# A hybrid decoder step on one core: order of the first loads, and who turns the sample rows

## The reference, cut to what matters

```python
def rms_norm(x, g):
    y = xf * lax.rsqrt(jnp.mean(xf * xf, axis=-1, keepdims=True) + RMS_EPS)
    return (y * g).astype(x.dtype)

h = rms_norm(xp, norm_g[l])                  # xp: 512 x 2048; the same for xs: 8 x 2048
z = jnp.einsum('btd,de->bte', h, w_in)       # w_in: 2048 x 6144
u, gp, q, k, v, ga = split(z)
pm = pool_mix(u, ...)                        # trailing means, a 256 x 256 map for each group
a = dilated_attn(q, k, v, ...)               # 16 heads of 64
xp = xp + concat(pm * silu(gp), a * silu(ga)) @ w_out
y = rms_norm(xp, final_norm_g)
```

## Time and profile before

| what | before |
|---|---|
| three runs, us | 821.51, 822.56, 828.95 |
| median, us | 822.56 |
| the profiled execution: its time, its span, us | 821.09, 819.3 |
| TensorE busy in the span | 807.1 us, 99% |
| VectorE, ScalarE, GpSimd busy | 77%, 49%, 25% |
| mean granted TensorE clock | 0.996 |

### The profile page before, as it was taken

One profiled execution on the slowest core, in us unless ns is written; L12 is line 12 of the kernel. 1 busy time (PEld: TensorE's weight loads), 2 busy tenths in 40 slices (PEclk: granted clock), 3 DMA queues, 4 the chain that ended last, 5 costly groups with the idle time before them and its releaser, 6 DMA issues.

```text
span 819.3 us, 17483 instructions
## 1 busy us (share of the span) xinstructions
PE 807.1 (99%) x6625; PEld 802.6 (98%) x6625; DVE 627.4 (77%) x1347; ACT 398.9 (49%) x875; POOL 203.2 (25%) x340
## 2 busy tenths in 40 slices
PE   9999999999999999999999999999999999999995
PEld 8999999999999999999999999999999999999994
DVE  4657895897589778958885897689888886777765
ACT  4745435533554454345435533553465345555554
POOL 2103502520360045014402610450000131222220
PEclk9999999999999999999999999999999999999998
DMA  8569647856774696578558756884668567766565
GB/s 297 142 173 232 168 125 171 231 144 168 188 208 122 163 233 169 152 175 228 152 141 186 204 147 182 193 214 123 172 195 272 156 181 203 207 184 174 150 180 218
DMA packets 271499, 150.04 MB, mean 183 GB/s; under 512 B 44448, under 2 KB 261472, under 8 KB 271392
## 3 DMA queue, kind: packets, MB, share of 16 engines
q1 hardware_dynamic: 239784, 118.97, 53.7%
q0 software_dynamic: 12672, 20.59, 9.9%
q10 hardware_dynamic: 18960, 9.38, 4.0%
HBM read 119.49 MB, written 28.27 MB: 180 GB/s over the span
## 4 chain that ended last, share of the span: by engine, by line
PE 87%; DVE 6%; DMA 3%; issue 1%; ACT 1%; SPq 1%; POOL 1%; DVEq 0%; ACTq 0%
PE pj L889 64%; PE pj L1048 13%; PE ps_s L946 1%; PE ps_s L948 1%; PE ps_o L977 1%; PE ps_o L975 1%; DMA out<-arena 1%; PE ps_o L889 1%; DVE w_lo L1624 1%; PE ps_t L995 1%; PE ps_s L995 1%; PE ps_s L889 1%; PE ps_s L827 1%; DVE arena L1755 1%; DMA w_raw<-in_w_out 0%
## 5 line engine op out<-in xcount | busy, mean ns | idle before, releaser
L889 PE MATMUL pj<-mov_hi,w_hi 128*128 128x260 f32 (+1 forms) x1632 | 332.1, 285 | 0.3 <-DVE mov_lo L1645 0.3
L889 PE MATMUL pj<-mov_hi,w_lo 128*128 128x260 f32 (+1 forms) x1632 | 328.3, 283 | 0.0
L889 PE MATMUL pj<-mov_lo,w_hi 128*128 128x260 f32 (+1 forms) x1632 | 327.8, 282 | 0.0
L889 PEld LDWEIGHTS pj<-mov_hi,w_hi 128*128 128x128 f32 x1632 | 252.7, 189 | 2.1 <-issue 0.6
L889 PEld LDWEIGHTS pj<-mov_lo,w_hi 128*128 128x128 f32 x1632 | 251.4, 188 | 0.0
L889 PEld LDWEIGHTS pj<-mov_hi,w_lo 128*128 128x128 f32 x1632 | 251.4, 188 | 0.0
L1148 ACT ACTIVATE w_hi<-w_raw 128x640 fp32r<-128x640 f32 (+1 forms) x157 | 121.4, 773 | 228.5 <-PE pj L889 159.3
L1624 DVE TENSOR_TENSOR w_lo<-w_raw,w_hi 128x640 fp32r<-128x640 f32 (+1 forms) x157 | 135.5, 863 | 62.7 <-ACT w_hi L1148 62.3
L1566 POOL DMA_DIRECT2D p_scratch<-extra x168 | 104.8, 631 | 82.4 <-DVE extra L1727 79.9
L1597 POOL DMA_DIRECT2D y_scratch<-arena x56 | 37.6, 678 | 110.5 <-DVE arena L2209 81.3
L1540 POOL DMA_DIRECT2D out<-arena x8 | 4.6, 569 | 213.0 <-DMA arena<-arena 213.0
(11 more groups left out here) (275 smaller groups left out, 1295.3 us busy)
## 6 DMA issues: line engine op xcount, KB each, us to landing
w_raw<-in_w_in SPq DMA_DIRECT2D x96, 320.0 KB, 4.1
w_raw<-in_w_in SPq DMA_DIRECT2D x48, 384.0 KB, 4.5
arena<-in_cache_k_win SPq DMA_DIRECT2D x16, 384.0 KB
arena<-in_cache_v_win SPq DMA_DIRECT2D x16, 384.0 KB
p_scratch<-extra POOLq DMA_DIRECT2D x112, 48.0 KB, 3.3
w_raw<-in_w_out SPq DMA_DIRECT2D x26, 192.0 KB, 3.0
arena<-in_cache_k_win SPq DMA_DIRECT2D x8, 512.0 KB
arena<-in_cache_v_win SPq DMA_DIRECT2D x8, 512.0 KB
```

Source lines behind the costliest of these rows:

```text
L889: mm = pe.matmul(dst[h][:, 0:own.stop - own.start], w, m[:, k, own], start=(k == 0 and i == 0), stop=(c == 2 and k == KT - 1 and i == 2))
```

## The change

Four things are changed, all of them in the opening.

1. Loads on SyncE: x piece 0 goes first. x is cut into eight pieces (1, 1, 2, 2, 2, 2, 3, 3 k's). Weight chunk 0 comes in two transfers, k's 0 and 1 with a semaphore of their own (`first_in`), k's 2 to 5 on `raw_in[0]`. Chunk 1 stands behind x piece 4, chunk 2 behind piece 6. The plain rows `x_smp` (which only a sum of squares needs in step 1) come last.
2. The gains and the samples are loaded by ScalarE's queue. The samples go into a block of zeros `smp_blk` (written by GpSimd) in four transfers that place 32-element pieces so that one VectorE transpose by 32x32 blocks gives all 16 k's turned (`smp_t`). TensorE's 16 sample transposes are gone.
3. On ScalarE and VectorE the samples' split now stands behind that of k = 0, not ahead of it.
4. On TensorE there are 7 + 2 + 3 + 2 matmuls on zeros where there were 11 + 2 + 8, some of them now between the turns of k = 0 and k = 1. k's 2, 3 are turned after the product of k = 1, k's 4, 5 after that of k = 2, and then x of k + 3 after the product of k.

Four semaphores of a later stage are used for the two added x pieces, for `first_in` and for `smp_in`; the later waits count 16 more (`mov_count`).

```diff
-        x_cols = tuple(P * k for k in (0, 2, 4, 6, 10, 13, 16))
+        x_at = (0, 1, 2, 4, 6, 8, 10, 13, 16)
+        x_cols = tuple(P * k for k in x_at)
...
-            sp.dma_start(ident, consts[:, C_ID:C_ID + P]).then_inc(id_in, 16)
-            sp.dma_start(g_rows[0:KT, :], norm_g[0].rearrange("(k p) -> k p", p=P)).then_inc(g_in, 16)
-            sp.dma_start(x_smp[0:NB, :], xs).then_inc(xs_in, 16)
-            for c in range(XP):
+            def load_x(c):
                 cols = slice(x_cols[c], x_cols[c + 1])
                 sp.dma_start(x_nat[:, :, cols], xp[:, :, cols]).then_inc(x_in[c], 16)
-                if c % 2 == 0:
-                    load_chunk(c // 2)
+
+            load_x(0)
+            sp.dma_start(ident, consts[:, C_ID:C_ID + P]).then_inc(id_in, 16)
+            sp.dma_start(w_raw[:, 0, 0:2, :], wi[:, 0:2, COL_OF[0]:COL_OF[0] + P]).then_inc(first_in, 16)
+            load_x(1)
+            sp.dma_start(w_raw[:, 0, 2:CK, :],
+                         wi[:, 2:CK, COL_OF[0]:COL_OF[0] + P]).then_inc(raw_in[0], 16)
+            for c in (2, 3, 4):
+                load_x(c)
+            load_chunk(1)
+            for c in (5, 6):
+                load_x(c)
+            load_chunk(2)
+            load_x(7)
+            sp.dma_start(x_smp[0:NB, :], xs).then_inc(smp_in, 16)
...
-            keep_busy(11)
+            keep_busy(7)
...
-            pe.wait_ge(xs_in, 16)
-            for k in range(KT):
-                tr = pe.transpose(ps_o[:, NB * k:NB * k + NB], x_smp[0:NB, P * k:P * k + P],
-                                  ident[0:NB, 0:NB])
-            tr.then_inc(g_turned, 1)
...
-                    if n == 0 and k == 1:
-                        for i in range(2, 6):
-                            turn_x(i)
-                    if n < 3 and 2 <= k < KT - 4:
-                        turn_x(k + 4)
+                    if n == 0 and k in (1, 2):
+                        turn_x(2 * k)
+                        turn_x(2 * k + 1)
+                    if n < 3 and 3 <= k < KT - 3:
+                        turn_x(k + 3)
...
-                    for k in range(2):
-                        turn_x(k)
-                    keep_busy(8)
+                    turn_x(0)
+                    keep_busy(3)
+                    turn_x(1)
+                    keep_busy(2)
...
+            act.dma_start(g_rows[0:KT, :], norm_g[0].rearrange("(k p) -> k p", p=P)).then_inc(g_in, 16)
+            act.wait_ge(sq_pm, 1)
+            smp = xs.rearrange("b (k q c) -> q b k c", q=SQS, c=SQ)
+            for a in range(SQS):
+                act.dma_start(smp_blk[SQ * a:SQ * a + NB, :].rearrange("b (k c) -> b k c", c=SQ),
+                              smp[a]).then_inc(xs_in, 16)
...
+            pool.memset(smp_blk, 0.0).then_inc(sq_pm, 1)
...
+            dve.wait_ge(xs_in, 16 * SQS)
+            dve.transpose(smp_t, smp_blk).then_inc(g_turned, 1)
```

More of the change, by code:

```diff
@@ L244, in layer_step @@
         x_smp = take(D_MODEL)
-        junk_a = [take(SEQ) for _ in range(2)]
+        smp_blk, smp_t = take(SEQ), take(SEQ)
         junk_l = [take(D_MODEL), x_smp]
@@ L354, in layer_step @@
         x_banks = (pj[1][0], pj[1][1], ps_s, ps_t)
-        x_cols = tuple(P * k for k in (0, 2, 4, 6, 10, 13, 16))
-        x_part = (0,) * 2 + (1,) * 2 + (2,) * 2 + (3,) * 4 + (4,) * 3 + (5,) * 3
+        x_at = (0, 1, 2, 4, 6, 8, 10, 13, 16)
+        x_cols = tuple(P * k for k in x_at)
         XP = len(x_cols) - 1
-        x_then_quarter = [sem(f"x_then_quarter{i}") for i in range(XP)]
-        x_in = x_then_quarter
+        x_part = tuple(c for c in range(XP) for _ in range(x_at[c], x_at[c + 1]))
+        x_then_quarter = [sem(f"x_then_quarter{i}") for i in range(6)]
+        mov_in = {i: sem(f"mov_in{i}") for i, k in enumerate(OUT_K) if k in STAGED}
+        x_in = x_then_quarter + [mov_in[3], mov_in[4]]
+        first_in, smp_in = mov_in[5], mov_in[6]
         X_IN = 16
@@ L422, in layer_step @@
         stg_hi_done, stg_split, stg_st = sem("stg_hi_done"), sem("stg_split"), sem("stg_st")
-        mov_in = {i: sem(f"mov_in{i}") for i, k in enumerate(OUT_K) if k in STAGED}
         kn_st, vn_st, us_st, up_st = sem("kn_st"), sem("vn_st"), sem("us_st"), sem("up_st")
@@ L565, in pv_at, with mov_count @@
             return p.s[h] + (6 if p is FINAL else 9)
+        def mov_count(i):
+            return 32 + 16 * (i in (3, 4, 5, 6))
         def own_other(h):
@@ L879, in chunk @@
                         if k in mov_in:
-                            pe.wait_ge(mov_in[k], 32)
+                            pe.wait_ge(mov_in[k], mov_count(k))
                         else:
@@ L1168, in _ @@
                                scale=g_t[:, k:k + 1]).then_inc(x_hi_done, 1)
+                if k == 0:
+                    act.wait_ge(xg_done, 1)
+                    act.activation(mov_hi[:, :, SEQ:NT], xg_smp.rearrange("p (k b) -> p k b", k=KT),
+                                   ACT.Copy).then_inc(x_hi_done, 1)
                 if k < 2:
                     own = slice(0, 2) if k == 0 else slice(2, CK)
-                    act.wait_ge(raw_in[0], 16)
+                    act.wait_ge(first_in if k == 0 else raw_in[0], 16)
                     act.activation(w_hi[:, 0, own, :], w_raw[:, 0, own, :],
@@ L1453, in _ @@
                 if step == 1:
-                    act.wait_ge(g_turned, 2)
+                    act.wait_ge(smp_in, 16)
                     act.activation(x_smp[0:NB, :], x_smp[0:NB, :], ACT.Square,
@@ L1637, in _ @@
             xg = xg_smp.rearrange("p (k b) -> p k b", k=KT)
-            dve.tensor_tensor(xg, ps_o[:, 0:NB * KT].rearrange("p (k b) -> p k b", k=KT),
+            dve.tensor_tensor(xg, smp_t.rearrange("p (k c) -> p k c", c=SQ)[:, :, 0:NB],
                               g_t.unsqueeze(2).to_broadcast([P, KT, NB]), ALU.mult).then_inc(xg_done, 1)
-            dve.wait_ge(x_hi_done, 1)
-            dve.tensor_tensor(mov_lo[:, :, SEQ:NT], xg, mov_hi[:, :, SEQ:NT].bitcast(F32),
-                              ALU.subtract).then_inc(x_lo_done, 1)
             for k in range(KT):
-                dve.wait_ge(x_hi_done, k + 2)
+                dve.wait_ge(x_hi_done, k + 1 + (k > 0))
                 dve.scalar_tensor_tensor(out=mov_lo[:, k, 0:SEQ], in0=x_banks[k % 4][:, :],
@@ L1648, in _ @@
                                          op1=ALU.subtract).then_inc(x_lo_done, 1)
+                if k == 0:
+                    dve.wait_ge(x_hi_done, 2)
+                    dve.tensor_tensor(mov_lo[:, :, SEQ:NT], xg, mov_hi[:, :, SEQ:NT].bitcast(F32),
+                                      ALU.subtract).then_inc(x_lo_done, 1)
                 if k < 2:
@@ L2127, in whole_x @@
                         dve.wait_ge(m_split, after_split(r))
-                    dve.wait_ge(mov_in[3], 32)
+                    dve.wait_ge(mov_in[3], mov_count(3))
                     dve.wait_ge(pooled_split, PAIRS)
@@ L2132, in whole_x @@
                     for r in range(KQ, 2 * KQ):
-                        dve.wait_ge(mov_in[r], 32)
+                        dve.wait_ge(mov_in[r], mov_count(r))
                     dve.wait_ge(av_sum, PAIRS)
```

5 lines of the change are left out of this document (1 added, 4 removed).

## The result

The changed kernel is slower: 828.68 us median of 20 runs (826.40 to 833.86) against 822.88 us (821.39 to 829.01, 20 runs), ratio 1.0063 with a 95% interval of 1.0045 to 1.0081. The forecast was 821.8 with a range up to 824.2, so it had the sign wrong: 5.8 us of loss in place of 0.8 us of gain. The profiled execution took 833.1 us, among the slowest of the 20; its span is 831.3 us against 819.3, so this pair of profiles lies 12.0 us apart and not 5.8.

A forecast was written before the change was run, and what follows sets the result against it. TensorE's own work was taken to bound the kernel. An earlier end of the first products, with three ahead and loads costing 0, gave 0.8 us gain: 822.56 - 0.8 = 821.8 us against the median, range 819.7 to 824.2.

The forecast's parts named there:

- What bounds: After the opening only TensorE's work sets the pace, 0.38 us slack; opening shifts reach the end nearly one for one.
- the yardstick: Traces: start of ScalarE's write of rstd_bc. Prediction: products of k = 0, 1 break even ending at 11.05 us.
- The samples' landing: Opening, ScalarE's queue: last sample transfer lands at 4.7 to 6.1 us, taken as 5.6; first product at 8.1.
- The slower rival: Late samples delay the first product; loss starts from landing at 7.05 us, 1.5 us at 8.5 (time 824); chance 0.15.
- the issue: ScalarE issues four sample transfers at 0.41 us each, from 1.55 to 3.2 us, the last at 2.8.
- The memset: GpSimd's zeroing of the 128x512 sample block takes 0.8 us, from 0.75 to 1.55 us, before the sample transfers.
- The clock: TensorE's pace in the first twelve products: gain 1.4 us if high, 0.3 if rising late, -0.5 if low throughout.
- Three ahead: Turning x of k + 3 in TensorE's stream leaves 0.65 us spare; cost 0 to 0.2 us, taken as 0.
- gain = 11.05 - E: E is the end of the products of k = 0 and 1; the formula already charges 0.89 us for two turns.
- the signs of failure: VectorE before its transpose beyond 7 us, 250 ns matmuls after 11 us, or mov_lo idle at every k.
- x in order costs nothing and gains nothing: SyncE's reordered x loads change nothing beyond the first turns, since those wait for TensorE, not data.
- the identity behind x piece 0: Identity, second on SyncE, lands at 3.7 us, leaving TensorE idle 0.75 us after seven matmuls on zeros.

The follow-up runs named there:

- with the queues held: Changed kernel, SyncE issuing x piece 1 and all later loads only after the four sample transfers landed; one profiled execution, 824.49 us.
- the bridge: Changed kernel with 20 matmuls on zeros instead of 2 behind the turn of k = 1; 829.1 us, ratio 1.0074.
- the split behind: Kernel before with the samples' split behind that of k = 0 and 4 matmuls on zeros instead of 8; 827.05 us, ratio 0.9999.
- the version with smaller pieces, without the two costs and with the identity first again: Changed kernel with plain sample rows turned by TensorE, four ahead, identity before x piece 0; 824.12 us, ratio 0.9999.

## Why the prediction was wrong

**What bounds.** Right as far as the times can tell. A stream made 4.0 us late was 4.5 (2.3 to 6.8) late at the end, and the change stands 5.6 us up at the yardstick of the first profiles and 5.8 in the medians. But the 0.38 us of slack in the earlier trace rows were those of one execution: another of the same kernel has a wait of 2.1 us at 114 us, and the two kernels' first profiles lie 12.0 us apart at the end, with 5.6 from the opening.

**The samples' landing: the step that failed.** I took 5.6 us from a range of 4.7 to 6.1, and measured 9.53 and 10.21. Two terms were mis-sized. The larger is the time from the last issue to the landing: 2.8 taken, 5.50 measured. Its bounds came from the identity, the first transfer of all, and from the median of 112 small ones in the middle of the kernel, a line whose transfers took from 2.0 to 6.7 us. They held for transfers with little beside them: with the queues held it is 2.31 us, right between the 1.9 and 3.3 of the earlier trace rows. But these pieces stood beside the heaviest traffic of the kernel. The profile of before shows x landing 4 us apart there, which I used for x alone, and its loads of x in the first 20 us took far more than 3.3:

```profile
arena<-in_x_prompt SPq DMA_DIRECT2D x3, 512.0 KB, 6.5
```

The same traffic held up x: that of k = 2 and 3 landed at 9.81, not at the 8.2 I had worked out from bytes, at no cost since TensorE was waiting for the samples. Here the rule of the Trainium skill (DMA: Bandwidth & Descriptors, Specifications) spoke against the change, and its side was right; the reason that the runs show is less the time of the small piece itself (12.7 ns beside the traffic, 12.5 without) than its wait for the engines that it shares with pieces of 512 bytes to 1.5 KB. No run here shows the read-modify-write. The slower rival named this mechanism, with the decision point at a landing of 7.05 us, and got 0.15 where it should have led.

The smaller term is the issue. The four issues of ScalarE (shortest, median and longest in ns, start of the first and the last in us):

```profile
L1175 ACTq DMA_DIRECT2D arena<-in_x_sample x4: 683/686/1279, 1.3 to 4.0; - x4
```

The first took 1.28 us and the others 0.69, not 0.41 each, so the last began at 4.03 where I had 2.8. The memset took 0.53 and not 0.8, which gave back 0.3. Together 1.2 us of issue and 2.7 of landing make the 3.9 by which the samples were late.

**The clock.** I had the cases right (high at once, as before, low throughout: 9.65, 10.7, 11.1 for the end of the twelve products) but took each for a start at 8.1 after an idle time of 0.5 us. After a wait of 4.9 us the low level lasted beyond the twelve products; with zeros in the wait it was over by about 8.3 us. Worth: 1.33 + 0.42 = 1.75 us in the rows, 1.70 by the bridge.

**Three ahead.** The 0.89 us of the two turns were right; "cost 0 to 0.2, I take 0" was wrong. From the start of k = 2 to the yardstick, five kernels three ahead need 27.25 or 27.26 us and seven four ahead 25.20 to 25.44, so 1.8 to 2.06 us, some 0.9 to 1.2 of them beyond the two turns. Four profiles stand apart: the changed kernel's second, at 28.8 with its late clock, and three of four ahead in which the turn of k = 6 waits for x (the second and third of before, at 27.33 and 25.86, and the one with the split behind, at 25.75). I had reckoned the spare time in the steady part only. The stalls that I can place lie at its ends: at k = 4, where little is ahead yet, and at k = 15, where VectorE turns to the next chunk's weights only after the last x.

**The sum, redone.** The formula gain = 11.05 - E gives 11.05 - 15.27 = -4.2 with the measured E. With the slow turn (0.42) and the unforeseen stalls (27.26 - 25.43 - 0.89 = 0.94) it is -5.6, the measured shift. So the yardstick held and the terms put into it did not. Against the forecast gain of 0.8 that is a miss of 6.4 us: 4.2 by the first product (8.1 forecast, 12.33 measured: the samples 3.9 late, and 2.8 us from their landing to it in place of 2.5), 0.8 by the twelve products (2.94 in place of about 2.15), 0.4 by the slow turn and 0.9 by three ahead. Two of the signs of failure came as the prediction named them: VectorE before its transpose until 9.56, and slow matmuls after 11 us.

**The loads.** "x in order costs nothing and gains nothing" held for x as far as the times tell, though the turn of k = 6 waited for the large piece of x by 1.65 us in the second profile of before and by 0.2 in the third, and never in a kernel with x in smaller pieces. That the identity behind x piece 0 would be late was forecast as 3.7 us, measured 3.69 in the changed kernel; but with plain sample rows beside it, it was 4.9. The change's loads show no gain of their own: the version with smaller pieces, without the two costs and with the identity first again is equal to before, and with x piece 0 first it stands 1.7 us higher at the yardstick.

**Range and chances.** Within 1% was right, and hardly hard. The range was too narrow above since the samples' landing was bounded by two rows of transfers in quieter places, and the rival that had it later was priced at 824 with a landing at 8.5.

## What to carry to other kernels

The same four transfers landed 2.3 to 7.0 us after the last issue in these runs, by what was beside them. So bound a transfer's landing by transfers of the same stretch, and ask what else is on the engines before a critical small transfer is cut into small pieces. Before an engine is relieved of work in an opening, look at what its new supplier waits for: here 1.8 us of narrow transposes on TensorE gave way to a wait of 4.9, and the wait cost twice, once as time and once because the clock rose later. This pipeline's depth had its price at its two ends, so count the turns that fill the first latency and what the last step shares its engine with.

## What the runs showed of the hardware

The page's granted clock reads 1.00 in the first microseconds while 260-column matmuls take 250 ns; the pace of the matmuls tells the level there, the column does not. It can read 1.00 even over the twelve slow products, as here with four ahead in the changed kernel, behind an idle time of 3.8 us:

```profile
11.82:14.76 2.94, 2.94 (x13) 1.00 1.10 380
```

By the pace, the rise came at another time from run to run of the same kernel: about 10.3 us in the first and third profile of before, while the samples were turned (4.8 to 6 us) in the second. It came between about 5 and 12 us in the nine profiles in which TensorE had no wait over 0.8 us between 1.2 us and the rise, at about 12 and 13 in the two with a wait of 1.8 to 1.9 us for the identity, at 13 with 2.7 us in the run with the queues held, and at 17 to 22 in the four with 3.8 to 5.1 us. Once up, 1.8 us of idle time left it up; no trace here has a longer one at the high level. After the long wait it took 5 us of products in one execution of the changed kernel and about 9 in the other (12.6 to 21.5 us), where the column agrees with the pace:

```profile
12.60:20.00 7.40, 6.55 (x29) 0.50 1.09 362
20.00:21.00 1.00, 1.00 (x6) 0.50 0.72 148
21.00:22.00 1.00, 1.00 (x7) 0.52 0.11 31
22.00:23.00 1.00, 1.00 (x11) 1.00 0.00 0
```

(The changed kernel, second profile, TensorE by stretch: busy, clock, DMA share, GB/s.) VectorE's split of the samples took 0.28 us in one run and 0.72 in the profile of the changed kernel, there beside a GpSimd square of x:

```profile
11.17 0.72 DVE L1670 TENSOR_TENSOR mov_lo<-arena,mov_hi 128x128 fp32r<-128x128 f32 x1
```

```profile
11.13 0.61 POOL L1547 TENSOR_TENSOR arena<-arena 128x256 f32<-128x256 f32 x1 [0.71 <-DMA arena<-in_x_prompt]
```

They overlap from 11.17 to 11.74. That the one slows the other was not tried by itself. What makes TensorE wait 1 to 3 us at the first heads in some executions stays open too, and with it whether it has a part in the difference of the two kernels.
